# Expert routing with split one-hot products, slot weights as factors by partition, and six weight slabs fetched early

## The chip, the cores and the metric

One core of one Trainium2 chip runs the whole program in one launch. The metric is the device time of an execution in microseconds (us). A hardware profile of one execution comes with it.

## What is computed

Two transformer-like blocks on 512 tokens of 1024 channels, all float32. The change concerns one step of the first, the expert-choice feed-forward:

```python
def expert_choice_ffn(n, w_router, w_gate, w_up, w_down):
    cap = EC_FACTOR * L // N_EXPERTS                      # 64 of 512 tokens for each of 16 experts
    aff = jax.nn.softmax(jnp.einsum('bld,de->ble', n, w_router), axis=-1)
    vals, idx = lax.top_k(jnp.swapaxes(aff, 1, 2), cap)
    xs = jax.vmap(lambda hb, ib: hb[ib])(n, idx)          # gather
    a = jnp.einsum('becd,edf->becf', xs, w_gate)
    u = jnp.einsum('becd,edf->becf', xs, w_up)
    y = jnp.einsum('becf,efd->becd', jax.nn.silu(a) * u, w_down) * vals[..., None]
    return zeros(L, D).at[idx].add(y)                     # scatter
```

Before it stands a mixer with recurrences, behind it a norm and two layers of a second block (feed-forward, attention, feed-forward), which the change leaves alone.

## The kernel before, in words

The program is a row of stages, each a block with one instruction stream for each engine and a barrier behind it. Buffers hold 128 partitions; a tile of the token-major or channel-major activations is 128 x 512. Weights come as slabs of 128 x 2048 float32 (1 MiB), issued by SyncE. The function `experts` makes four stages of the feed-forward step:

- `route`: TensorE multiplies with the router (L104), VectorE makes the softmax and finds each expert's 64 tokens by eight rounds of maximum and replacement (L1426, L1427), and leaves in `slot_of` the slot of every token. SyncE loads the router and the tables for the later rotary embedding.
- `pick`: TensorE turns the normed activations to token-major form (L1488, 32 transposes), ScalarE copies them out as `x_tok` (L1470). VectorE compares slot numbers (L1442), which gives `pick`, a one-hot matrix of tokens by expert slots, and GpSimd multiplies it by the affinities (L1460), which gives `weighed`. Then the gather: 16 products of four float32 matmuls (L104 with `experts_work`), evicted in turn by VectorE and ScalarE into `xs`. Then 32 transposes of `weighed` (L1504) make `put`, by which the scatter multiplies.
- `experts`: eight pairs of experts, twelve slabs each, 96 in all, through a ring of eight slots. Gate and up (L1543), a transpose of the hidden tile (L1553), down (L1567), for two experts at a time in two halves of the array's columns. SyncE issues slab n when the pair of slabs eight before has been used (L1528). ScalarE evicts the result (L1589).
- `scatter`: for each of eight channel tiles eight float32 matmuls of `y` by `put` (L104), VectorE adds the tile to the residual (L1635), ScalarE squares it and GpSimd folds the squares (L156, L166) for the norm stage `final` that follows.

In the profile's names `experts_work` is the work buffer `m.work`, `mix_mixed` is lent for `xs`, and ring slots are `mix_ring` (4), `mix_normed` (2, the space of the normed activations) and `experts_work` (2). Where a float32 product is split, as in the feed-forward and projection stages, ScalarE writes a rounded copy of the operand in type fp32r (`hi`), VectorE subtracts it from the original (`lo`), and one matmul is made with each.

Of the kernel before, what the change touches and what calls it, by code (L numbers as in the profile page):

```python
# [14 lines left out]
F32 = mybir.dt.float32  # L15
# [7 lines left out]
P = 128  # L23
# [10 lines left out]
SG = 2  # L34
# [1330 lines left out]
def experts(nc, m, io):  # L1365


    w = m.work
    pick, weighed = cut(w, 0, NT, NE * CAP), cut(w, 4096, NT, NE * CAP)
    x_tok, put = cut(w, 8192, NT, D), cut(w, 12288, NE // 2, T)  # L1370
    small = 16384
    affinity, slot_of = cut(w, small, NT, NE), cut(w, small + 64, NT, NE)
    router = cut(w, small + 128, KD, NE)
    peak, total = cut(w, small + 256, NT), cut(w, small + 260, NT)
    top = cut(w, small + 264, 8)[0:NE]
    rest, chosen, ones_row, count = (cut(w, small + 288 + T * i, T)[0:NE] for i in range(4))
    xs = m.mixed[:, :, :].rearrange("p a b -> p (a b)").rearrange("p (k s) -> p k s", k=KD)
# [58 lines left out]
    with stage(nc, m, "pick") as (block, sem):  # L1436
        turned, copied, picked, weighted, gathered, put_done, freed, put_read = sem(8)

        @block.vector
        def _(dve):  # L1440
# [5 lines left out]
            for n in range(16):  # L1446
                dve.wait_ge(gathered, n + 1)
                k, half = divmod(n, 2)
                if n % 2 == 0:
                    dve.tensor_copy(xs[:, k, half * T:(half + 1) * T], m.ps[:, 4 + n % 4, :])\  # L1450
                        .then_inc(freed, 1)
            for pair in range(0, NE // 2, 2):
                dve.wait_ge(put_done, pair + 1)
                dve.tensor_copy(put[:, pair, :], m.ps[:, pair % 4, :]).then_inc(put_read, 1)

        @block.gpsimd
        def _(pool):
            for t in range(NT):
                pool.wait_ge(picked, t + 1)
                pool.tensor_tensor(weighed[:, t, :].rearrange("p (e s) -> p e s", e=NE),  # L1460
                                   pick[:, t, :].rearrange("p (e s) -> p e s", e=NE),
# [20 lines left out]
        def _(pe):  # L1482
            for n in range(8):
                if n >= 4:
                    pe.wait_ge(copied, n - 3)
# [1396 lines left out]
```

## Time and profile before

| | |
|---|---|
| median of 3 runs | 3973.25 us (3958.51, 3973.25, 3974.38) |
| profiled execution | 3963.0 us, of it the span 3961.1 us |
| TensorE busy | 3397.4 us, 86% of the span |
| VectorE, ScalarE, GpSimd busy | 1731.5, 1035.2, 268.6 us |
| granted TensorE clock, mean | 0.927 |
| DMA | 326.24 MB, mean 82 GB/s |

Times in rows are from the span's start. A float32 matmul leaves two records in the profile, an fp32r matmul one. PEclk is the granted TensorE clock as a share of 2.4 GHz. The records of matmuls overlap, so the pace of a burst is read from the starts. The idle time at a row's end was closed by the engine and line named behind it.

### The profile page before, as it was taken

To read this page: it belongs to the slowest core of one execution; us is meant where nothing else is said; L and a number is where in the kernel's file an instruction comes from. 1 tells how busy PE (TensorE), PEld (TensorE's weight loads), DVE (VectorE), ACT (ScalarE), POOL (GpSimd) and SP (SyncE) were. 2 spreads that over 40 slices of the span, in tenths; PEclk is the share of its full clock that TensorE was granted. 3 is DMA by queue.
4 is the path that set the end of the run, shared out by engine and by line. 5 is a ranking of instruction groups with operands and counts; after the bars stand their busy time and mean duration, and the time that the engine had idled before them with its cause. 6 is when DMAs were issued, how large, how long until landed. Compare 5 with 4: busy or idle time off the path is not lost. (4 is left out here: it accounts for less than half of the span.)

```text
span 3961.1 us, 39195 instructions
## 1 busy us (share of the span) xinstructions
PE 3397.4 (86%) x15298; PEld 2414.1 (61%) x15298; DVE 1731.5 (44%) x2473; ACT 1035.2 (26%) x1475; POOL 268.6 (7%) x230
## 2 busy tenths in 40 slices
PE   4988986768787778699978889999899798889997
PEld 3465665333463223588856457888788675557886
DVE  2747757464533000444234654442443235645433
ACT  2121221120321000422132453221322223443222
POOL 1110010020111000000001100000000102000001
PEclk6999998889888999799989899999999999899998
DMA  1101000101101993222121012221322121013221
GB/s 74 61 25 43 11 11 1 54 10 44 74 24 43 420 420 136 89 100 99 64 96 70 1 43 96 95 96 64 118 96 95 52 97 59 1 43 117 96 98 60
DMA packets 49390, 326.24 MB, mean 82 GB/s; under 512 B 6896, under 2 KB 7280, under 8 KB 11120
## 3 DMA queue, kind: packets, MB, share of 16 engines
q1 hardware_dynamic: 49264, 324.52, 21.7%
q8 instruction: 84, 1.38, 0.1%
q14 instruction: 42, 0.34, 0.0%
HBM read 321.35 MB, written 2.10 MB: 82 GB/s over the span
## 5 line engine op out<-in xcount | busy, mean ns | idle before, releaser
L358 PE MATMUL psum<-ffn_x_hi,ffn_w_hi 128*128 128x512 f32 x1408 | 551.4, 392 | 13.8 <-DVE ffn_x_lo L314 13.8
L358 PE MATMUL psum<-ffn_x_lo,ffn_w_hi 128*128 128x512 f32 x1408 | 550.9, 391 | 0.0
L358 PE MATMUL psum<-ffn_x_hi,ffn_w_lo 128*128 128x512 f32 x1408 | 550.5, 391 | 0.0
L303 DVE TENSOR_TENSOR ffn_w_lo<-ffn_raw,ffn_w_hi 128x2048 fp32r<-128x2048 f32 x128 | 293.4, 2292 | 420.8 <-ACT ffn_w_hi L274 420.8
L104 PE MATMUL psum<-mix_normed,mix_ring 128*128 128x512 f32 x832 | 373.9, 611 | 64.8 <-DMA mix_ring<-w_ssd 32.0
L274 ACT ACTIVATE ffn_w_hi<-ffn_raw 128x2048 fp32r<-128x2048 f32 x128 | 245.2, 1916 | 573.0 <-PE psum L358 573.0
L104 PEld LDWEIGHTS psum<-mix_normed,mix_ring 128*128 128x128 f32 x832 | 162.6, 197 | 273.3 <-issue 230.5
L358 PEld LDWEIGHTS psum<-ffn_x_hi,ffn_w_hi 128*128 128x128 f32 x1408 | 266.4, 189 | 75.2 <-DVE ffn_w_lo L310 20.0
L358 PEld LDWEIGHTS psum<-ffn_x_hi,ffn_w_lo 128*128 128x128 f32 x1408 | 266.1, 189 | 55.8
L358 PEld LDWEIGHTS psum<-ffn_x_lo,ffn_w_hi 128*128 128x128 f32 x1408 | 266.2, 189 | 55.6
L358 PE MATMUL psum<-ffn_hid_hi,ffn_w_hi 128*128 (+1 forms) x704 | 273.9, 389 | 0.0
L358 PE MATMUL psum<-ffn_hid_lo,ffn_w_hi 128*128 (+1 forms) x704 | 273.9, 389 | 0.0
L358 PE MATMUL psum<-ffn_hid_hi,ffn_w_lo 128*128 (+1 forms) x704 | 273.9, 389 | 0.0
L329 DVE TENSOR_TENSOR ffn_lift<-psum,squares_sb 128x512 f32<-128x512 f32 x88 | 60.8, 691 | 316.0 <-PE psum L358 316.0
L358 PEld LDWEIGHTS psum<-ffn_hid_hi,ffn_w_hi 128*128 128x128 f32 x704 | 132.1, 188 | 27.6
L358 PEld LDWEIGHTS psum<-ffn_hid_lo,ffn_w_hi 128*128 128x128 f32 x704 | 132.1, 188 | 27.5
L358 PEld LDWEIGHTS psum<-ffn_hid_hi,ffn_w_lo 128*128 128x128 f32 x704 | 132.1, 188 | 27.2
L624 DVE SCALAR_TENSOR_TENSOR recurrences_work<-psum,mix_group_cols,recurrences_work 128x509 f32<-128x509 f32 (+2 forms) x216 | 143.2, 738 | 0.0
L409 PE MATMUL psum<-mix_out_s_hi,mix_out_w_hi 128*128 128x512 f32 x256 | 103.0, 403 | 39.8 <-DVE mix_out_w_lo L460 39.8
L166 POOL TENSOR_TENSOR squares_sb<-squares_sb,ffn_gates 128x512 f32<-128x512 f32 x28 | 35.9, 1283 | 1457.2 <-ACT ffn_gates L156 1453.7
L409 PE MATMUL psum<-project_x_hi,project_w_hi 128*128 128x512 f32 x240 | 95.0, 396 | 46.2 <-DVE project_x_lo L1801 46.2
L292 ACT ACTIVATE ffn_hid_hi<-ffn_lift 128x512 f32 (+1 forms) x88 | 55.6, 632 | 267.7 <-DVE ffn_lift L333 267.7
(426 smaller groups left out, 5255.9 us busy)
## 6 DMA issues: line engine op xcount, KB each, us to landing
ffn_raw<-w_ffn SPq DMA_DIRECT2D x128, 1024.0 KB, 4.8
mix_ring<-w_experts SPq DMA_DIRECT2D x48, 1024.0 KB, 13.7
mix_ring<-w_mix SPq DMA_DIRECT2D x36, 1024.0 KB, 4.9
mix_normed<-w_experts SPq DMA_DIRECT2D x24, 1024.0 KB, 14.7
experts_work<-w_experts SPq DMA_DIRECT2D x24, 1024.0 KB, 15.7
mix_ring<-w_gdn SPq DMA_DIRECT2D x16, 1024.0 KB, 4.8
mix_ring<-w_ssd SPq DMA_DIRECT2D x10, 1024.0 KB, 6.9
mix_ring<-w_out SPq DMA_DIRECT2D x8, 1024.0 KB, 6.5
```

The lines of the kernel that those rows point to most:

```text
L104: ins = pe.matmul(out, weights(k), moving(k), start=(k == 0), stop=(k == n - 1))
L166: pool.tensor_tensor(m.squares, m.squares, tmp[:, k % 2, :], ALU.add).then_inc(folded, 1)
L274: act.activation(w_hi[:, q, :], raw[:, q, :], ACT.Copy).then_inc(hi_done, 1)
L292: act.activation(hid_hi[:, n, :], lift, ACT.Copy).then_inc(hid_hi_done, 1)
L303: dve.tensor_tensor(w_lo[:, q, :], raw[:, q, :], w_hi[:, q, :].bitcast(F32), ALU.subtract)\
L329: dve.tensor_tensor(lift, m.ps[:, 2 * q + 1, :], rstd, ALU.mult).then_inc(taken, 1)
L358: ins = pe.matmul(out, wp[:, q, w], xp, start=start and a == 0, stop=stop and a == 2)
L409: pe.matmul(out, a[0], b[0], start=start, stop=False)
L624: ins = dve.scalar_tensor_tensor(d[:, lo:hi], s[:, lo + shift:hi + shift], col[:, tap:tap + 1], d[:, lo:hi], ALU.mult, ALU.add)
```

## The change

1. `pick` and `put` are of type fp32r. The gathered activations are split: ScalarE's copy is `x_hi` (fp32r), VectorE subtracts to make `x_lo`, and the gather makes two fp32r matmuls where one float32 matmul stood. The scatter does the same with `y`, one channel tile at a time through two buffers, `y_hi` and `y_lo`.
2. GpSimd's weighting goes. `put` is the transpose of the bare one-hot matrix, and its transposes stand between the gather's products. The slot weights come from 32 float32 matmuls with two moving columns each, and become the factor `weight` of ScalarE's eviction in `experts`.
3. Slabs 0 to 3 are fetched in `route`, slabs 4 and 5 in `pick`, each with a semaphore of its own (`m.early`); the last two ring slots are a buffer that exists from `experts` on. The other 90 slabs are fetched in `experts` as before.
4. Memory: `m.mixed` lives only through the first mixer; the four stages get buffers of their own in place of the work buffer.

```diff
@@ -1365,16 +1365,25 @@
-    w = m.work
-    pick, weighed = cut(w, 0, NT, NE * CAP), cut(w, 4096, NT, NE * CAP)
-    x_tok, put = cut(w, 8192, NT, D), cut(w, 12288, NE // 2, T)
...
+    big = picking.enter_context(nc.sbuf_tensor("experts_pick", [P, 3 * 4096], F32R))
+    pick, x_hi, x_lo = (cut(big, 4096 * n, NT, NE * CAP) for n in range(3))
+    put = cut(m.moe_put, 0, NE // 2, T)
...
+    weight = cut(small, 6 * T, NE // 2)
+    xs = cut(m.moe_xs, 0, KD, NE * CAP)
+    spare = m.xT[:, :, :].rearrange("p k t -> p (k t)")
+    ring = [m.ring[:, s, :] for s in range(SLOTS)] + [spare[:, s * SLAB:(s + 1) * SLAB] for s in range(2)]
+    n_early = len(ring)
+
+    def fetch(sp, n):
+        sp.dma_start(ring[n], io["w_experts"][n]).then_inc(m.early[n], 16)
@@ -1384,6 +1393,8 @@
+            for n in range(SLOTS):
+                fetch(sp, n)
             sp.wait_ge(tables, 16)
@@ -1434,7 +1445,13 @@
     with stage(nc, m, "pick") as (block, sem):
...
+            sp.wait_ge(turned, 8)
+            for n in (4, 5):
+                fetch(sp, n)
@@ -1443,74 +1460,90 @@
                                   ALU.is_equal).then_inc(picked, 1)
+                for half in range(2):
+                    n, at = 2 * t + half, slice(half * T, (half + 1) * T)
+                    dve.wait_ge(hi_done, n + 1)
+                    dve.tensor_tensor(x_lo[:, t, at], m.ps[:, n % 4, :], x_hi[:, t, at].bitcast(F32), ALU.subtract)\
+                        .then_inc(split, 1)
...
+            dve.wait_ge(weighed, 1)
+            for e in range(2):
+                rows = slice(e * CAP, (e + 1) * CAP)
+                both = m.ps[rows, 4, 0:NE].rearrange("p (i e) -> p i e", e=2)
+                dve.tensor_copy(weight[rows], both[:, :, e])
-        @block.gpsimd
-        def _(pool):
-            for t in range(NT):
-                pool.wait_ge(picked, t + 1)
-                pool.tensor_tensor(weighed[:, t, :].rearrange("p (e s) -> p e s", e=NE),
...
             for n in range(8):
                 if n >= 4:
-                    pe.wait_ge(copied, n - 3)
+                    pe.wait_ge(split, n - 3)
...
-            pe.wait_ge(copied, 8)
+            pe.wait_ge(split, 8)
             pe.wait_ge(picked, NT)
             for n in range(16):
...
-                product(pe, m.ps[:, 4 + n % 4, :], lambda t: x_tok[:, t, tok(k)],
-                        lambda t: pick[:, t, half * T:(half + 1) * T], NT).then_inc(gathered, 1)
+                for t in range(NT):
+                    for part in (x_hi, x_lo):
+                        ins = pe.matmul(m.ps[:, 4 + n % 4, :], part[:, t, tok(k)], pick[:, t, half * T:(half + 1) * T],
+                                        start=(t == 0 and part is x_hi), stop=(t == NT - 1 and part is x_lo))
+                ins.then_inc(gathered, 1)
+                if n >= 5 and n % 2:
+                    turn_picks((n - 5) // 2)
+            turn_picks(6)
+            turn_picks(7)
+            pe.wait_ge(read_v, 7)
             for pair in range(NE // 2):
...
+                ins = product(pe, m.ps[:, 4, 2 * pair:2 * pair + 2], lambda t: pick[:, t, tok(pair)].bitcast(F32),
+                              lambda t: affinity[:, t, 2 * pair:2 * pair + 2], NT)
+            ins.then_inc(weighed, 1)
@@ -1522,7 +1555,7 @@
-            for n in range(12 * pairs):
+            for n in range(n_early, 12 * pairs):
                 if n >= slots:
@@ -1586,7 +1622,8 @@
-                    ins = act.activation(y[:, i, half * T:(half + 1) * T], m.ps[:, 5 + half, :], ACT.Copy)
+                    ins = act.activation(y[:, i, half * T:(half + 1) * T], m.ps[:, 5 + half, :], ACT.Copy,
+                                         scale=weight[:, i:i + 1])
@@ -1610,12 +1647,19 @@
         @block.scalar
         def _(act):
+            for k in range(KD):
+                if k >= 2:
+                    act.wait_ge(done, k - 1)
+                act.activation(y_hi[:, k % 2, :, :], y[:, :, tok(k)], ACT.Copy).then_inc(hi_done, 1)
             square_tiles(act, m, sq, renewed, squared, folded)
@@ -1625,14 +1669,28 @@
             for k in range(KD):
-                product(pe, m.ps[:, k, :], lambda pair: y[:, pair, tok(k)], lambda pair: put[:, pair, :],
-                        NE // 2).then_inc(done, 1)
+                pe.wait_ge(split, k + 1)
+                for pair in range(NE // 2):
+                    pe.matmul(m.ps[:, k, :], y_hi[:, k % 2, pair, :], put[:, pair, :], start=(pair == 0), stop=False)
+                    ins = pe.matmul(m.ps[:, k, :], y_lo[:, k % 2, pair, :], put[:, pair, :], start=False,
+                                    stop=(pair == NE // 2 - 1))
+                ins.then_inc(done, 1)
...
+            for k in range(KD):
+                dve.wait_ge(hi_done, k + 1)
+                dve.tensor_tensor(y_lo[:, k % 2, :, :], y[:, :, tok(k)], y_hi[:, k % 2, :, :].bitcast(F32),
+                                  ALU.subtract).then_inc(split, 1)
+                if k:
+                    add(k - 1)
+            add(KD - 1)
```

How it moves instructions, at three places. TensorE in `pick`, from the transposes of the activations to the stage's end, before:

```order
L65 UNCONDITIONAL_BRANCH
L1481 UNCONDITIONAL_BRANCH
L1488 MATMUL psum<-const_sb,mix_normed 128x128 x32
L104 MATMUL psum<-experts_work 128x512 x64
L1504 MATMUL psum<-const_sb,experts_work 128x128 x32
L65 UNCONDITIONAL_BRANCH
```

and with the change:

```order
L1503 UNCONDITIONAL_BRANCH
L1517 MATMUL psum<-const_sb,mix_normed 128x128 x32
L1527 MATMUL psum<-experts_pick 128x512 x48
L1509 MATMUL psum<-const_sb,experts_pick 128x128 x4
L1527 MATMUL psum<-experts_pick 128x512 x16
L1509 MATMUL psum<-const_sb,experts_pick 128x128 x4
...
L1527 MATMUL psum<-experts_pick 128x512 x16
L1509 MATMUL psum<-const_sb,experts_pick 128x128 x12
L104 MATMUL psum<-experts_small,experts_pick 128x2 x32
L65 UNCONDITIONAL_BRANCH
L1563 UNCONDITIONAL_BRANCH
```

Of the 32 transposes of the one-hot matrix 20 now stand inside the gather and 12 behind it; the 64 products are 128 matmuls, and 32 small ones close the stage. L1517, L1527 and L1509 are the lines of the activations' transposes, the gather and the one-hot transposes; `experts_pick` holds `pick`, `x_hi` and `x_lo`; the rows left out repeat the two above them.

SyncE from the router's transfer on, before:

```order
L1385 DMA experts_work<-w_router 128x128
L1386 DMA const_sb<-const_f 128x2304
L65 UNCONDITIONAL_BRANCH
L1523 UNCONDITIONAL_BRANCH
L1528 DMA mix_ring<-w_experts 128x2048 x4
```

and with the change:

```order
L1394 DMA experts_small<-w_router 128x128
L1395 DMA const_sb<-const_f 128x2304
L1385 DMA mix_ring<-w_experts 128x2048 x4
L65 UNCONDITIONAL_BRANCH
L1450 UNCONDITIONAL_BRANCH
L1385 DMA mix_normed<-w_experts 128x2048 x2
L65 UNCONDITIONAL_BRANCH
L1556 UNCONDITIONAL_BRANCH
L1561 DMA experts_slabs<-w_experts 128x2048 x2
```

Six slab transfers now stand ahead of the `experts` stage, four of them in `route`.

ScalarE in `scatter`, before and with the change:

```order
L1589 ACTIVATE experts_work<-psum 128x512 x4
L65 UNCONDITIONAL_BRANCH
L1617 UNCONDITIONAL_BRANCH
L156 ACTIVATE squares_sb<-resid_sb 128x512
L156 ACTIVATE mix_norm_tmp<-resid_sb 128x512 x7
```

```order
L1625 ACTIVATE experts_y<-psum,experts_small 128x512 x4
L65 UNCONDITIONAL_BRANCH
L1657 UNCONDITIONAL_BRANCH
L1662 ACTIVATE experts_y_hi<-experts_y 128x1024 x8
L156 ACTIVATE squares_sb<-resid_sb 128x512
L156 ACTIVATE mix_norm_tmp<-resid_sb 128x512 x7
```

Eight rounded copies now stand ahead of all eight squares in its queue.

## Rows read from the trace of the kernel before

**Rows 1.** The page, what DMA moved in 40 equal slices of the span, GB/s.

```profile
GB/s 74 61 25 43 11 11 1 54 10 44 74 24 43 420 420 136 89 100 99 64 96 70 1 43 96 95 96 64 118 96 95 52 97 59 1 43 117 96 98 60
```

**Rows 2.** Stretches of one stage each: length, busy us (instructions) by engine, PEclk, DMA share, GB/s.

```profile
1171.10:1206.60 35.50, 15.46 (x72) 14.60 (x72) 16.55 (x36) 1.54 (x2) 0.00 (x0) 0.50 0.10 36
1207.40:1275.00 67.60, 64.48 (x192) 33.40 (x192) 16.34 (x16) 11.63 (x20) 10.36 (x4) 0.97 0.00 0
1275.88:1523.90 248.02, 181.69 (x800) 64.22 (x800) 11.04 (x16) 14.74 (x25) 0.00 (x0) 0.98 0.98 406
1524.80:1584.50 59.70, 56.87 (x128) 24.83 (x128) 5.53 (x8) 5.03 (x8) 8.88 (x7) 0.97 0.00 0
```

**Rows 3.** Timeline of TensorE in pick: start us, us, line, what, count, idle before.

```profile
1207.47 5.81 PE L1488 MATMUL psum<-const_sb,mix_normed 128*128 128x128 f32 x32 [1.22 <-PEq L67]
1215.66 55.17 PE L104 MATMUL psum<-experts_work 128*128 128x512 f32 x128 [2.38 <-DVE experts_work L1442]
1270.67 3.66 PE L1504 MATMUL psum<-const_sb,experts_work 128*128 128x128 f32 x32
```

**Rows 4.** Timeline of SyncE and TensorE in experts.

```profile
1275.88 1.98 SPq L1528 DMA_DIRECT2D mix_ring<-w_experts  x4
...
1283.20 8.92 PE L1543 MATMUL psum<-mix_ring,mix_mixed 128*64 128x512 f32 x32 [8.87 <-DMA mix_ring<-w_experts]
1294.59 3.65 PE L1543 MATMUL psum<-mix_normed,mix_mixed 128*64 128x512 f32 x16 [2.47 <-DMA mix_normed<-w_experts]
...
1519.12 3.65 PE L1567 MATMUL psum<-experts_work 128*64 128x512 f32 x16 [1.28 <-DMA experts_work<-w_experts]
```

**Rows 5.** Timeline of scatter: TensorE, VectorE's last addition, GpSimd's last fold.

```profile
1524.85 56.87 PE L104 MATMUL psum<-experts_work 128*128 128x512 f32 x128 [2.08 <-PEq L67]
...
1581.76 0.69 DVE L1635 TENSOR_TENSOR resid_sb<-psum,resid_sb 128x512 f32<-128x512 f32 x1 [6.18 <-PE psum L104]
...
1583.19 1.26 POOL L166 TENSOR_TENSOR squares_sb<-squares_sb,mix_norm_tmp 128x512 f32<-128x512 f32 x1 [5.60 <-ACT mix_norm_tmp L156]
```

**Rows 6.** Timeline of TensorE in the projection, first and last of 39 fp32r matmuls.

```profile
2084.72 0.39 PE L409 MATMUL psum<-project_x_hi,project_w_hi 128*128 128x512 f32 x1
...
2093.33 0.39 PE L411 MATMUL psum<-project_x_hi,project_w_lo 128*128 128x512 f32 x1
```

**Rows 7.** The same kind at the start of a feed-forward stage, nine steps apart.

```profile
1620.52 0.63 PE L358 MATMUL psum<-ffn_x_hi,ffn_w_lo 128*128 128x512 f32 x1
...
1624.36 0.63 PE L358 MATMUL psum<-ffn_x_hi,ffn_w_lo 128*128 128x512 f32 x1
```

**Rows 8.** Single lines of code: durations ns min/median/max, first and last start, shapes.

```profile
L443 ACT ACTIVATE mix_out_s_hi<-mix_mixed x8: 1039/1061/1061, 1054.0 to 1131.3; 128x1024 fp32r<-128x1024 f32 x8
...
L457 DVE TENSOR_TENSOR mix_out_s_lo<-mix_mixed,mix_out_s_hi x8: 1218/1226/1226, 1055.1 to 1132.4; 128x1024 fp32r<-128x1024 f32 x8
...
L1442 DVE TENSOR_TENSOR experts_work<-const_sb,experts_work x4: 1217/2072/2924, 1207.5 to 1212.6; 128x1024 f32<-128x1024 f32 x4
...
L185 ACT ACTIVATE resid_sb<-resid_sb,gains_sb x6: 704/705/721, 1585.4 to 3936.7; 128x512 f32<-128x512 f32 x6
```

**Rows 9.** Short stretches for the clock: one-column products, end of router products, transposes.

```profile
138.00:140.00 2.00, 2.00 (x16) 1.64 (x14) 0.00 (x0) 1.23 (x2) 0.00 (x0) 1.00 0.67 131
...
1184.00:1188.00 4.00, 3.40 (x16) 3.29 (x16) 0.45 (x2) 0.00 (x0) 0.00 (x0) 0.50 0.00 0
...
1211.00:1213.00 2.00, 2.00 (x16) 2.00 (x15) 2.00 (x2) 1.58 (x4) 2.00 (x2) 0.79 0.02 4
```

**Rows 10.** Timeline of TensorE: one-column products, the router's products.

```profile
138.55 1.84 PE L780 MATMUL psum<-const_sb,mix_ring 128*128 128x1 f32 x16
...
1173.56 13.83 PE L104 MATMUL psum<-experts_work,mix_normed 128*128 128x16 f32 x64 [14.47 <-DMA experts_work<-w_router]
```

**Rows 11.** Timeline of the stage final: ScalarE's first square, GpSimd's folds.

```profile
1597.67 0.63 ACT L156 ACTIVATE squares_sb<-resid_sb 128x512 f32<-128x512 f32 x1 [5.30 <-DVE resid_sb L205]
...
1598.97 9.70 POOL L166 TENSOR_TENSOR squares_sb<-squares_sb,mix_norm_tmp 128x512 f32<-128x512 f32 x7 [14.52 <-ACT mix_norm_tmp L156]
```

More of the change, by code:

```diff
@@ L1365, in experts @@
 def experts(nc, m, io):
-    w = m.work
-    pick, weighed = cut(w, 0, NT, NE * CAP), cut(w, 4096, NT, NE * CAP)
-    x_tok, put = cut(w, 8192, NT, D), cut(w, 12288, NE // 2, T)
[L1371 to L1377, printed above, removed]
+    small = m.moe_small
+    picking, slabs, parts = ExitStack(), ExitStack(), ExitStack()
+    big = picking.enter_context(nc.sbuf_tensor("experts_pick", [P, 3 * 4096], F32R))
+    pick, x_hi, x_lo = (cut(big, 4096 * n, NT, NE * CAP) for n in range(3))
+    put = cut(m.moe_put, 0, NE // 2, T)
+    affinity, slot_of = cut(small, 0, NT, NE), cut(small, 64, NT, NE)
+    router = cut(small, 128, KD, NE)
+    peak, total = cut(small, 256, NT), cut(small, 260, NT)
+    top = cut(small, 264, 8)[0:NE]
+    rest, chosen, ones_row, count = (cut(small, 288 + T * i, T)[0:NE] for i in range(4))
+    weight = cut(small, 6 * T, NE // 2)
[5 more added lines that the diff above has]
+        sp.dma_start(ring[n], io["w_experts"][n]).then_inc(m.early[n], 16)
     by_expert = lambda a: a.unsqueeze(2).to_broadcast([P, NT, NE])
@@ L1611, in _ @@
                 dve.tensor_copy(hid_t[:, i % 2, :], m.ps[:, 4, :]).then_inc(turned_read, 1)
+    parts.close()
+    y_hi, y_lo = (parts.enter_context(nc.sbuf_tensor(f"experts_y_{n}", [P, 2, NE // 2, P], F32R))[:, :, :, :]
+                  for n in ("hi", "lo"))
     with stage(nc, m, "scatter") as (block, sem):
-        done, renewed, squared, folded = sem(4)
+        hi_done, split, done, renewed, squared, folded = sem(6)
         sq = cut(m.norm_tmp, 0, 2, T)
@@ L1627, in _, with add @@
             for k in range(KD):
-                product(pe, m.ps[:, k, :], lambda pair: y[:, pair, tok(k)], lambda pair: put[:, pair, :],
-                        NE // 2).then_inc(done, 1)
+                pe.wait_ge(split, k + 1)
[4 more added lines that the diff above has]
+                ins.then_inc(done, 1)
         @block.vector
         def _(dve):
-            for k in range(KD):
+            def add(k):
                 dve.wait_ge(done, k + 1)
                 dve.tensor_tensor(m.resid[:, k, :], m.ps[:, k, :], m.resid[:, k, :], ALU.add).then_inc(renewed, 1)
+            for k in range(KD):
[5 more added lines that the diff above has]
+            add(KD - 1)
+    parts.close()
+    slabs.close()
 MLA_H, NSA_H, SB_H = 6, 6, 4
@@ L2560, in memory @@
     m.signals = [ctx.enter_context(nc.semaphore(f"signal_{i}")) for i in range(48)]
+    m.early = [ctx.enter_context(nc.semaphore(f"expert_slab_{i}")) for i in range(SLOTS + 2)]
     m.ps = ctx.enter_context(nc.psum_tensor("psum", [P, 8, T], F32))
```

95 lines of the change are left out of this document (51 added, 44 removed).

## Prediction

> **What bounds the kernel now.** I read the page first, then the stretches stage by stage, then the timeline of each engine in three stages. The page's row of slices [rows 1] shows 420 GB/s in two of 40 slices and nothing near it elsewhere: one stage streams weights, and it is `experts`. The stretches [rows 2] give four stages that the diff touches. In `route` (35.5 us) TensorE runs at 0.50 of its clock and DMA moves 36 GB/s, so the memory port is nearly free. In `pick` TensorE is busy 64.5 of 67.6 us, in `scatter` 56.9 of 59.7: both are TensorE's. In `experts` DMA is at 0.98 while TensorE is busy 182 of 248 us.
>
> The timelines say what the work costs. In `pick` [rows 3] 64 float32 products stand as 128 records (each instruction leaves two) and take 55.17 us, 0.862 us a product; GpSimd's four weightings (10.36 us [rows 2]) lie beside the transposes and the start. In `experts` [rows 4] TensorE needs 3.65 us for a pair of slabs, but from the third pair (1294.59) to the last (1519.12) lie 45 steps of 4.99 us, each ended by a landing. In `scatter` [rows 5] the 64 products take 56.87 us, and behind them hang one addition (0.69), one square and one fold (1.27); the tail ends at 1584.45.
>
> **The price of a split product.** The projection stage has the same form, own weights for every 128x512 fp32r matmul: 38 steps from 2084.72 to 2093.33 [rows 6], 0.2266 us each. Two of them do what 0.862 us did, so a product costs 0.453 us. At the low clock the step is 0.427 us (nine steps in 3.84 us, 1620.52 to 1624.36 [rows 7]).
>
> **Pick: 68.4 us before** (1207.47 to the first issue of `experts`, 1275.88). Added on VectorE are eight subtractions between the four comparisons. A comparison took 1.22 us where nothing ran beside it and up to 2.92 beside GpSimd's multiplications [rows 8], which go; a 128x512 VectorE operation takes 0.69 [rows 5]. 4 x 1.22 + 8 x 0.69 = 10.4, with hand-offs to ScalarE I take 11.3 us until the first product (before: 8.2). What is queued behind that wait on TensorE is the whole gather. Then 128 x 0.2266 = 29.0 us of products, and the 32 transposes that were there before, 3.7 us [rows 3], now mostly between products; the evictions of both, about 0.7 us each, are shared by VectorE and ScalarE while a product of the gather takes 1.8 us, and stay hidden. At the start TensorE has been short of work and may begin at 1.2 GHz: `scatter` before began so and took 56.87 us where `pick` took 55.17, so 1.7 us [rows 3, 5], with 0 and 3.4 as ends. The transposes of `pick` did raise the clock, to a mean of 0.79 in 1211 to 1213 [rows 9]. The Trainium skill ("TensorE: Matmul & The Clock Gate", PE-mode transpose) says the reverse, that the full clock does not engage for transposes; by that rule this term would be 3.4 us instead of 1.7, and the trace does not agree with it here.
>
> New on TensorE are 32 float32 products with two moving columns, the slot weights, 64 records. Nothing covers them: the stage ends behind them. Their cost is that of loading 128x128 weights. Sixteen one-column products took 1.84 us at clock 1.00, 0.115 each; the router's 64 records took 13.83 us at 0.50, 0.216 each, and did not lift the clock in all that time [rows 9, 10]. So 7.4 us if the clock stays, 13.8 if it falls at once. They follow dense work, so it starts at 2.4 GHz and should fall on the way: I take the middle, 10.6. Two small copies and the hand-over: 1.4. Sum 11.3 + 1.7 + 29.0 + 3.7 + 10.6 + 1.4 = 57.7, **a gain of 10.7 us**. Ends: weights -3.2 and +3.2, start -1.7 and +1.7, comparisons still at their old median of 2.07 us +3.4, transposes in the stream somewhat dearer +1.2.
>
> **Experts: 249 us before.** Six slabs, three pairs, are in place when the stage starts, and the port has 45 pairs left for 48: -3 x 4.99 = -15.0 us [rows 4]. Cover for the six: four go out behind the router's and the rope tables' transfers in `route`, 10 us of port in a stage of 35.5 us whose port is idle after the tables [rows 2]; nothing in the stage waits for them, and the router's transfer stands ahead of them in the queue, so I charge 0 (at worst some 2 us). Two go out in `pick` after the eighth transpose group, with some 45 us of TensorE's work ahead. If that cover were gone, TensorE would wait at 4.99 us a pair as before. New is a possible hole: slabs 6 and 7 take the port for 5 us, slab 8 waits for the first pair's use. Before, two pairs took 8.92 us from the low clock, so the first 5.3 [rows 4]; reuse then comes at about the time at which the port runs dry. I charge 0.5 us, ends 0 and 3. An activation with a factor by partition takes 0.71 us [rows 8]; two stand behind the last pair, and I charge 0.2 us more than for plain ones. **Gain 14.3 us.** The Trainium skill ("DMA: Bandwidth & Descriptors", Where 436 GB/s comes from) puts the HBM side at about 358 GB/s; by that a slab would take 2.9 us and the six would be worth 17.6 us. The page's rows say 420 [rows 1], that is 2.5 us, and I go by them.
>
> **Scatter: 59.6 us before** (1524.85 to 1584.45). Before the first product now stand ScalarE's rounded copy, 1.06 us, and VectorE's subtraction, 1.23, on exactly these shapes [rows 8]: 2.5 with hand-offs. Then 29.0 us, and 2.0 for the low clock: TensorE ends at 33.5. Each tile is 3.63 us of TensorE. Its conversion starts when the tile two before is done and takes 2.5 us, VectorE's addition fits in between: hidden, slack 1.1 us. But ScalarE's squares stand behind all eight copies in its queue. The last copy is released with the sixth tile, at 33.5 - 7.3 = 26.2, and ends at 27.4. Then all eight squares and seven folds run in a row, as in the `final` stage, 1597.67 to 1608.67, 11.0 us [rows 11]: 38.4, and 0.5 more for folds beside VectorE: 38.9. So squares and folds, not products, end the stage, 2.7 us later than the old tail would. **Gain 20.7 us**, ends -2.5 and +2.7.
>
> **Sum.** 10.7 + 14.3 + 20.7 = 45.7 us. The profiled execution took 3963.0 us, so 3917.3 by itself. The runs shown lie on both sides of it (median 3973.25, 10.3 above); all four average 3967.3, and the forecast is taken from there: **3921 us**. The terms' bad ends together leave a gain of 32 us, the good ones 54; from the slowest run (3974.4) and the fastest (3958.5) that gives 3942 and 3904, the range. It takes in the two faster rivals below.
>
> **Rivals.**
> *Conversions bound the scatter* (chance 0.07). If copy and subtraction did not hide under the other tile, each of seven further tiles would add 2.5 us: 17.5, so 3939. For it: two buffers only, and VectorE's additions lie in the same queue. Against it: the slack of 1.1 us by rows 8.
> *The early slabs buy nothing* (0.06). If the port runs dry at the stage's start and stays behind, or the early fetches only move waiting: 14.3 us lost, 3936. The diff alone would allow it; the order of SyncE shows six issues ahead of the stage, and the rows show an idle port.
> *Products stay at 1.2 GHz* (0.03). If the gaps before both bursts kept the clock down, 256 x (0.427 - 0.227) = 51 us would be lost [rows 6, 7]: 3972, no change. Against it: the old bursts reached 0.97 on average over their stages [rows 2].
> *Slower: the one-hot operand forces the slow pace* (0.02). All 256 new matmuls take one fp32r operand and an fp32r one-hot matrix. If one operand made them run as float32, each would cost 0.862 instead of 0.227: 163 us more, 4084. It becomes slower than before by over 0.5% from 0.48 us a matmul on ((46 + 20) / 256 above 0.227). In the projection both operands are fp32r as well, and run at 0.227, which speaks against it.
> The forecast itself has 0.78; 0.04 is left for the first two together or something unseen, about 3950.
>
> **Chances.** About 0.5% (20 us) is what a measurement of this kernel can tell from no change. Below 3953 lie the forecast, the first two rivals and most of the remainder: 0.94. Within: 0.04. Slower: 0.02.
>
> **What would show it.** In the changed kernel's profile: fp32r records of `pick` and `scatter` 0.227 us apart; the first gather product some 11 us after the stage's start; the 64 small records in 7 to 14 us with the clock falling below 1.00; the first three pairs of `experts` with no wait, then steps of 4.99 us for 42 more and a stage some 14 us shorter; in `scatter` a VectorE subtraction always ended before the tile that needs it, and GpSimd's seven folds in a row ending some 5 us behind the last product. Wrong would be: products 0.43 us apart, waits of TensorE on the subtraction in `scatter`, a landing awaited in the first three pairs, or a first router product much later in `route` than now, 2.5 us after its start (1173.56 against 1171.10 [rows 2, 10]).

## The result, and the profile after

| | before | after |
|---|---|---|
| median | 3970.2 us (4 runs, 3958.51 to 3974.38) | 3914.91 us (4 runs, 3911.68 to 3919.42) |
| ratio | | 0.9867, 95% interval 0.9849 to 0.9885 |
| profiled execution | 3963.0 us | 3912.02 us, of it the span 3910.2 us |

The changed kernel is faster, by 1.3%. The prediction was 3921 us with a range of 3904 to 3942, and its forecast case came true. The stretches of the changed kernel, cut at the stages as in [rows 2], come first; the columns are length, busy time of the five engines with their instructions, granted clock, DMA share and GB/s. The stages are `route`, `pick`, `experts`, `scatter`.

```profile
1171.10:1206.60 35.50, 15.46 (x72) 14.60 (x72) 16.57 (x36) 1.54 (x2) 0.00 (x0) 0.50 0.39 154
1207.40:1262.90 55.50, 50.80 (x256) 44.12 (x256) 17.95 (x26) 11.52 (x20) 0.00 (x0) 0.87 0.10 39
1263.77:1498.60 234.83, 182.05 (x800) 64.48 (x800) 11.04 (x16) 16.17 (x25) 0.00 (x0) 0.99 0.97 402
1499.50:1538.20 38.70, 31.68 (x128) 25.18 (x128) 15.25 (x16) 13.09 (x16) 8.96 (x7) 0.93 0.00 0
```

`route` has its old length of 35.5 us although its DMA rate went up to 154 GB/s. `pick`, `experts` and `scatter` are shorter, and GpSimd has nothing left to do in `pick`. Measured from the stage's first transpose to the next stage's first slab issue, from there to ScalarE's first copy, and from there to the first scaling of the stage `final` (L185), the three take 56.28, 235.75 and 39.61 us, together 331.64. Before it was 377.96 us (1207.47 to 1585.43). So 46.3 us were saved there; the prediction had 45.7.

`pick`, in the timelines of TensorE and VectorE:

```profile
1207.49 4.91 PE L1517 MATMUL psum<-const_sb,mix_normed 128*128 128x128 f32 x24 [1.25 <-PEq L67]
...
1217.84 12.81 PE L1527 MATMUL psum<-experts_pick 128*128 128x512 f32 x48 [4.01 <-DVE experts_pick L1466]
1230.49 0.60 PE L1509 MATMUL psum<-const_sb,experts_pick 128*128 128x128 f32 x4
1230.84 3.93 PE L1527 MATMUL psum<-experts_pick 128*128 128x512 f32 x16
...
1251.02 1.47 PE L1509 MATMUL psum<-const_sb,experts_pick 128*128 128x128 f32 x12
1252.33 10.15 PE L104 MATMUL psum<-experts_small,experts_pick 128*128 128x2 f32 x64
```

```profile
1210.71 1.22 DVE L1459 TENSOR_TENSOR experts_pick<-const_sb,experts_small 128x1024 fp32r<-128x1024 f32 x1
1211.84 1.28 DVE L1466 TENSOR_TENSOR experts_pick<-psum,experts_pick 128x512 fp32r<-128x512 f32 x2
```

The gather's burst starts 10.35 us after the stage's start, released by VectorE's last subtraction. From there to the weights' products nothing is awaited. The 48 matmuls at the start take 12.65 us to the next record where 48 at the later pace of 0.2333 take 11.2. At the end the 64 small records take 10.15 us.

`experts` and SyncE's first issues in it:

```profile
1263.97 9.98 PE L1579 MATMUL psum<-mix_ring,experts_xs 128*64 128x512 f32 x32 [1.48 <-PEq L67]
1273.77 3.61 PE L1579 MATMUL psum<-mix_normed,experts_xs 128*64 128x512 f32 x16
1277.20 3.61 PE L1579 MATMUL psum<-experts_slabs,experts_xs 128*64 128x512 f32 x16
1280.63 7.22 PE L1579 MATMUL psum<-mix_ring,experts_xs 128*64 128x512 f32 x32
...
1289.19 3.65 PE L1579 MATMUL psum<-mix_normed,experts_xs 128*64 128x512 f32 x16 [0.75 <-DMA mix_normed<-w_experts]
...
1493.63 3.65 PE L1603 MATMUL psum<-experts_slabs,experts_small 128*64 128x512 f32 x16 [1.24 <-DMA experts_slabs<-w_experts]
```

```profile
1263.77 0.81 SPq L1561 DMA_DIRECT2D experts_slabs<-w_experts  x2
1270.54 4.24 SPq L1561 DMA_DIRECT2D mix_ring<-w_experts  x4
```

A pair of slabs is 16 matmuls. TensorE runs through six pairs without waiting for a landing; the seventh, at 1289.19, is the first that waits, and from there to the last pair lie 41 steps of 4.986 us, the pace of [rows 4]. The first slab of a reused place is issued at 1270.54, 6.8 us into the stage.

`scatter` by TensorE, ScalarE and GpSimd:

```profile
1501.88 0.78 PE L1674 MATMUL psum<-experts_put,experts_y_hi 128*128 128x512 f32 x1 [4.60 <-DVE experts_y_lo L1687]
1502.46 0.63 PE L1675 MATMUL psum<-experts_put,experts_y_lo 128*128 128x512 f32 x1
...
1505.41 0.39 PE L1674 MATMUL psum<-experts_put,experts_y_hi 128*128 128x512 f32 x1
...
1532.47 0.40 PE L1674 MATMUL psum<-experts_put,experts_y_hi 128*128 128x512 f32 x1
```

```profile
1526.14 1.06 ACT L1662 ACTIVATE experts_y_hi<-experts_y 128x1024 fp32r<-128x1024 f32 x1 [2.67 <-PE psum L1675]
1527.10 0.61 ACT L156 ACTIVATE squares_sb<-resid_sb 128x512 f32<-128x512 f32 x1
...
1528.32 9.83 POOL L166 TENSOR_TENSOR squares_sb<-squares_sb,mix_norm_tmp 128x512 f32<-128x512 f32 x7 [359.25 <-ACT mix_norm_tmp L156]
```

The first product stands 2.36 us after the first copy. Up to 1505.41 the records are 0.43 us apart, then 116 steps to 1532.47 take 27.06 us, 0.2333 each. From the fourth on, each copy waits 2.67 us for a tile of products, so ScalarE waits for TensorE and not the other way round. The squares stand behind the last copy, and the folds end at 1538.15, some 4.6 us after the last product.

**The rest of the span.** It fell by 50.9 us and the stages account for 46.3. The other 4.6 us lie behind the stages, in code that the change leaves alone (2375.7 us before, 2371.1 after). Below, e10_both_moves and e11_changed_again show one stretch of it taking either of two times, 3.8 us apart, with the new kernel alone. Whether the change makes the shorter time likelier is not shown.

### The profile page after: what moved, and what is told of

It reads as the page before. It is cut to its first block and busy times, and to the rows that moved or that the text cites. A ratio compares the mean times of both kernels' runs of the same rounds, so it can differ in the third digit from the quotient of the medians.

```text
span 3910.2 us, 39337 instructions
## 1 busy us (share of the span) xinstructions
PE 3354.9 (86%) x15362; PEld 2423.3 (62%) x15362; DVE 1743.4 (45%) x2491; ACT 1044.5 (27%) x1483; POOL 258.2 (7%) x226
```

## The experiments

The three parts were undone one by one (e1 to e3), the weights' products were left out (e8), the conversion's cover was taken away (e6), the order of the two passes changed (e7), and two pieces of work moved to where the new profile had room (e4, e5, and both in e10). The kernels of e1 to e8 ran once each, e10 and e11 five times. Whole spans drift by up to 5.5 us ahead of the four stages and up to 12 behind them, so I compare the stages' lengths and not the times of the whole. "Pick, experts, scatter" are those between the events named above.

**e1_fetch_in_experts: the six slabs fetched when the stage starts.**

```diff
             for n in range(SLOTS):
-                fetch(sp, n)
...
-            for n in (4, 5):
-                fetch(sp, n)
...
+            for n in range(n_early):
+                fetch(sp, n)
             for n in range(n_early, 12 * pairs):
```

> The changed kernel with all 96 slab transfers issued in the experts stage (six no longer ahead of it); nothing else moves. If the early slabs save port time: the experts stage, from its first issue to the start of scatter, grows from 235.8 us to about 249 us, as before the change, each of 45 steps from the third pair on 4.99 us; route, pick and scatter stay within 0.5 us; total near 3925. If the early slabs only moved waiting: experts grows by less than 3 us. If the fetches in routing disturbed the router or the picking: route or pick gets shorter than 35.5 and 56.3 us.

Measured: 3931.08 us. Pick 56.32, experts 249.08, scatter 39.60.

```profile
1269.30 2.05 SPq L1385 DMA_DIRECT2D mix_ring<-w_experts  x4
```

```profile
1276.70 9.72 PE L1573 MATMUL psum<-mix_ring,experts_xs 128*64 128x512 f32 x32 [8.68 <-DMA mix_ring<-w_experts]
1286.69 3.65 PE L1573 MATMUL psum<-mix_normed,experts_xs 128*64 128x512 f32 x16 [0.26 <-DMA mix_normed<-w_experts]
```

Without the early slabs TensorE waits for the first landing again, and `experts` has its old 249 us, 13.3 more than in the changed kernel. `pick` and `scatter` move by less than 0.1 us. From the router's transfer to `pick` it is 36.59 us here (1176.39 to 1212.98) and 36.35 with the slabs behind that transfer (1171.14 to 1207.49). So the early fetch is worth 13.3 us and costs nothing in `route`.

**e2_gather_float32: the gather by float32 products, without the split.** The one-hot matrices, the weights' products and the early slabs stay.

```diff
...
-                        ins = pe.matmul(m.ps[:, 4 + n % 4, :], part[:, t, tok(k)], pick[:, t, half * T:(half + 1) * T],
-                                        start=(t == 0 and part is x_hi), stop=(t == NT - 1 and part is x_lo))
+                ins = product(pe, m.ps[:, 4 + n % 4, :], lambda t: x_hi[:, t, tok(k)].bitcast(F32),
+                              lambda t: pick[:, t, half * T:(half + 1) * T].bitcast(F32), NT)
...
```

> The changed kernel with the gather alone back to float32: one float32 copy of the activations, no subtraction, 64 float32 products (128 records). If the price of a product is all: products take 55.2 us instead of about 30.5 with their slow start, but begin at 6.8 us into the stage instead of 10.4; pick goes from 56.3 to about 78 us, the other stages stay. If the conversion work of VectorE had eaten much of the gain, pick would grow by clearly less than 20 us.

Measured: 3938.07 us. Pick 76.36, experts 234.40, scatter 40.48.

```profile
1217.29 20.87 PE L104 MATMUL psum<-experts_pick 128*128 128x512 f32 x48 [0.79 <-ACT experts_pick L1485]
1238.00 0.60 PE L1504 MATMUL psum<-const_sb,experts_pick 128*128 128x128 f32 x4
```

The first product stands 6.66 us after the stage's start instead of 10.35, since the subtractions are gone, but sixteen records take 7.03 us where the split pass has 3.93. The stage is 20.1 us longer. So the split of the gather alone is worth more than `pick` gained in all: the weights' products gave about 9 us back. `experts` is 1.35 us shorter here. Its first pair was used by 1292.36, 5.4 us into the stage instead of 6.8, and the section on the prediction compares the port behind it. `scatter` is 0.9 us longer, and nothing was changed in it.

**e3_scatter_float32: the scatter by float32 products.** Copy and subtraction of this stage go with it.

```diff
-                    pe.matmul(m.ps[:, k, :], y_hi[:, k % 2, pair, :], put[:, pair, :], start=(pair == 0), stop=False)
-                    ins = pe.matmul(m.ps[:, k, :], y_lo[:, k % 2, pair, :], put[:, pair, :], start=False,
-                                    stop=(pair == NE // 2 - 1))
+                product(pe, m.ps[:, k, :], lambda pair: y[:, pair, tok(k)], lambda pair: put[:, pair, :].bitcast(F32),
+                        NE // 2).then_inc(done, 1)
```

> The changed kernel with the scatter alone back to float32: no rounded copies, no subtractions, 64 float32 products. Scatter, from its start to the last fold, goes from 38.7 us back to 59.6; the tail behind the last product goes from 5 us to 2.7; pick and experts stay within 0.5 us. Rival (conversions bound the scatter): less than 17 us.

Measured: 3944.72 us. Pick 56.36; experts and scatter together 294.5 instead of 275.4 us.

```profile
1502.84 55.17 PE L104 MATMUL psum<-experts_put,experts_y 128*128 128x512 f32 x128 [2.26 <-PEq L67]
```

The burst is as long as the old one of `pick` [rows 3]: this time it ran at the full clock throughout. To the next stage, from 1502.84, it is 58.9 us; the changed kernel has 39.6 from its first copy. By the two stages together, the split scatter is worth 19.1 us.

**e8_no_weight_products: the 32 two-column products left out.** The slot weights are set to 1, so the part of the computation that weights the experts' outputs is missing.

```diff
-            dve.wait_ge(weighed, 1)
...
+            dve.memset(weight, 1.0)
...
-            pe.wait_ge(read_v, 7)
-            for pair in range(NE // 2):
-                ins = product(pe, m.ps[:, 4, 2 * pair:2 * pair + 2], lambda t: pick[:, t, tok(pair)].bitcast(F32),
-                              lambda t: affinity[:, t, 2 * pair:2 * pair + 2], NT)
-            ins.then_inc(weighed, 1)
```

> The changed kernel without the 32 small slot-weight products and the two copies behind them; the factor is set to 1, so this part of the computation is left out. Theory: pick shortens by the 10.2 us of the products and some 0.3 more, 56.3 to about 45.8; TensorE comes from dense work into experts, its first pair takes 3.7 to 5.3 us instead of 6.5, and the hole in the port closes, experts shorter by 1 to 1.6 us. Rival (the low clock at the start of experts comes from the stage change, not from the small products): pick shortens alike, experts stays at 235.8.

Measured: 3900.05 us. Pick 46.98, experts 235.23, scatter 39.47.

```profile
1254.06 1.47 PE L1505 MATMUL psum<-const_sb,experts_pick 128*128 128x128 f32 x12
1257.27 7.09 PE L1570 MATMUL psum<-mix_ring,experts_xs 128*64 128x512 f32 x32 [1.74 <-PEq L67]
```

The products cost 9.3 us of `pick`, and behind them the clock is low: here the first two pairs take 7.09 us instead of 9.98. Only 0.5 us of these 2.9 reach the end of `experts`, where 1 to 1.6 were expected: the stage's pace is that of the landings.

**e4_weights_in_gather: these products in the gather, ahead of its last two groups.**

```diff
+                if n == 13:
+                    pe.wait_ge(read_v, 7)
+                if n in (13, 14):
+                    for pair in range(4 * (n - 13), 4 * (n - 12)):
+                        ins = product(pe, m.ps[:, 4, 2 * pair:2 * pair + 2],
...
-            pe.wait_ge(read_v, 7)
-            for pair in range(NE // 2):
```

> The changed kernel with the 32 slot-weight products moved between the gather's last products (16 behind the fourteenth, 16 behind the fifteenth, into the bank that is free by then), the last product and twelve transposes behind them. If the price of the small products is their pace at the low clock: spread in two bursts of 3.7 us the clock holds, they cost 64 x 0.115 = 7.4 us instead of 10.2, pick goes from 56.3 to about 53.5, and experts starts at the high clock as without the products (first pair 3.6 us, stage 235.2). If the clock falls anyway between the bursts: pick 55 to 57, and the products behind them run at 0.43.

Measured: 3911.45 us. Pick 55.28, experts 234.96, scatter 40.35.

```profile
1250.28 3.63 PE L104 MATMUL psum<-experts_small,experts_pick 128*128 128x2 f32 x32
1253.77 2.09 PE L1527 MATMUL psum<-experts_pick 128*128 128x512 f32 x8
1255.70 3.81 PE L104 MATMUL psum<-experts_small,experts_pick 128*128 128x2 f32 x32
1259.37 3.50 PE L1527 MATMUL psum<-experts_pick 128*128 128x512 f32 x8
```

In two lots between dense work they take 7.44 us instead of 10.15: the clock was 1.00 up to 1259. But the eight dense matmuls behind the second lot took 3.50 instead of 2.09 us, so the low clock came a little later and its 1.4 us moved to them. `pick` won 1.0 us, `experts` 0.8 (first pair at full clock, its place reused 3.9 us into the stage), and `scatter` lost 0.7, because its slow start lasted longer (up to 1508.27, twelve records). Over the three stages 1.05 us are left.

**e5_squares_between: each tile's square between two copies.**

```diff
...
+                if k >= 2:
+                    square(k - 2)
+            square(KD - 2)
+            square(KD - 1)
-            square_tiles(act, m, sq, renewed, squared, folded)
```

> The changed kernel with ScalarE's squares placed between its rounded copies in scatter (square of tile k-2 behind the copy of tile k) instead of behind all eight. If the squares' place in the queue ends the stage: the last fold ends some 2.7 us behind the last product instead of 4.6, scatter from its start to the next stage goes from 39.6 to about 37.6 us, products unchanged. If folds or conversions bound it in another way: no change, or waits of TensorE on the subtraction.

Measured: 3926.94 us. Pick 56.90, experts 235.56, scatter 37.62.

```profile
1536.31 1.29 POOL L166 TENSOR_TENSOR squares_sb<-squares_sb,mix_norm_tmp 128x512 f32<-128x512 f32 x1 [1.70 <-ACT mix_norm_tmp L1663]
1540.04 1.26 POOL L166 TENSOR_TENSOR squares_sb<-squares_sb,mix_norm_tmp 128x512 f32<-128x512 f32 x1 [2.44 <-ACT mix_norm_tmp L1663]
```

`scatter` is 2.0 us shorter and ends, as the old one did, with one addition, one square and one fold behind the last product: each fold now waits for its square. So the row of squares and folds was what ended the stage, and the copies still come in time, 3.73 us apart as before. The whole took longer all the same (span 3925.2 us against 3910.2), which the shorter stages cannot cause: 4.7 of these 15.0 us lie ahead of `pick`, whose first transpose stands at 1212.20 instead of 1207.49, and 11.8 behind the stages. e10 has the same move in five executions.

**e6_one_buffer: one pair of buffers for hi and lo in the scatter instead of two.** The conversion of a tile has to wait for the products of the tile before: its cover is gone.

```diff
-                if k >= 2:
-                    act.wait_ge(done, k - 1)
-                act.activation(y_hi[:, k % 2, :, :], y[:, :, tok(k)], ACT.Copy).then_inc(hi_done, 1)
+                if k >= 1:
+                    act.wait_ge(done, k)
+                act.activation(y_hi[:, 0, :, :], y[:, :, tok(k)], ACT.Copy).then_inc(hi_done, 1)
...
```

> The changed kernel with one buffer instead of two for the split tile of the scatter: a tile's copy and subtraction start when the product before has ended. Theory (two buffers hide 2.4 us a tile): scatter grows by 7 x 2.4 = 17 us, from 39.6 to about 56, less up to 2 us by which squares and folds then keep up; the clock may fall in the gaps and add more. Rival (conversions were on the path already): it grows by clearly less than 10.

Measured: 3949.96 us. Pick 56.32, experts 235.70, scatter 61.99. The waits of 1503 to 1566 (who waited for whom: total, times, longest):

```profile
ACT experts_y_hi L1662 <- PE psum L1675: 41.6, 7, 6.8
PEld psum L1674 <- DVE experts_y_lo L1687: 25.4, 8, 5.5
PE psum L1674 <- DVE experts_y_lo L1687: 21.4, 8, 4.6
```

Now TensorE waits eight times for the subtraction, 21.4 us in all, and the stage is 22.4 us longer. Its copies stand 6.40 us apart instead of 3.73, so an uncovered conversion costs 2.67 us. Two of the six distances were 7.80 and 7.74, since the clock dropped there. That is 16.0 and 2.7 us; the other 3.7 come from the last copy, which has the squares behind it in the queue and now waits for the seventh tile instead of the sixth. Only the second pair of buffers keeps the split scatter ahead: without it the stage takes 62.0 us, longer than the float32 one (58.9 in e3, 60.6 before).

**e7_hi_then_lo: in the gather all hi products of a group, then all lo ones.** It asks whether the measured pace, a little over the one forecast, comes from hi and lo taking turns.

```diff
-                for t in range(NT):
-                    for part in (x_hi, x_lo):
+                for part in (x_hi, x_lo):
+                    for t in range(NT):
```

> The changed kernel with the gather's matmuls in another order: four with the rounded part, then four with the rest, so that the moving operand changes with every matmul. In the changed kernel split products stand 0.2333 us apart in gather and scatter, where the projection has 0.2266. If the pace comes from two matmuls in a row with the same moving operand: 0.2266 in the gather here, pick 0.9 us shorter (128 x 0.0067), scatter still 0.2333. If it comes from the operands' layout or type: 0.2333 in both.

Measured: 3918.38 us. Pick 56.53, experts 235.64, scatter 39.43.

```profile
1221.14 12.82 PE L1527 MATMUL psum<-experts_pick 128*128 128x512 f32 x48 [4.00 <-DVE experts_pick L1466]
...
1234.15 3.93 PE L1527 MATMUL psum<-experts_pick 128*128 128x512 f32 x16
```

From the first product to the weights' products it takes 34.50 us (1221.14 to 1255.64), in the changed kernel 34.49 (1217.84 to 1252.33). The order does not matter. What sets 0.2333 instead of 0.2266 us stays open; the operands' layout was not tried.

**e10_both_moves (e4 and e5 together) and e11_changed_again (the changed kernel), five executions each on one chip.**

> The weights' products stand inside the gather (as in e4) and each tile's square stands between two hi copies of the scatter (as in e5). Theory: the two stretches do not touch each other, so the savings of the single runs add: pick 55.3 instead of 56.3 us, experts about 235, scatter to the next stage about 37.6 to 38.4 instead of 39.6, in all 2.5 to 4 us below the changed kernel, a median near 3911 where the changed one of the same call has 3914, and still 1.3 to 1.5% below the kernel before. Rival A: the saving is taken back behind the scatter (as the mixer of the second block drifts by 4 to 8 us from run to run, it could also drown): the medians of the two then agree within 1 us although the four stages are shorter. Rival B: the squares between the copies make ScalarE late for the subtraction; then the scatter's products pause between tiles and the stage is not under 39 us.

> The changed kernel once more, on the chip of e10 and against the same runs of the kernel before: pick 56.3, experts 235.7, scatter 39.6 us, together 46 us shorter than before; ratio 0.985 to 0.989. If what the whole span gained beyond these 46 us (4.6 us in the profiled pair) belonged to the change, the median would again be over 50 us below the kernel before; if it is drift of one profiled pair, the medians differ by more or less than that from call to call.

Measured: e10 3915.31 us (3911.98 to 3920.14), ratio to before 0.9864 (0.9847 to 0.9881). e11 3917.84 us (3915.27 to 3920.07), ratio 0.9870 (0.9855 to 0.9886). The stages: e10 57.34, 235.41 and 37.50, sum 330.25 us; e11 56.28, 235.78 and 39.56, sum 331.62. The squares' 2.0 us came again. The weights' move gained nothing in `pick` this time, and `pick` was 1.1 us longer. Some 0.4 of it is a slower start of the gather (13.07 us for the first 48 matmuls instead of 12.65); and the low clock fell on the dense matmuls behind the second lot and on the last twelve transposes, which took 2.74 us instead of 1.47.

```profile
1253.59 3.95 PE L104 MATMUL psum<-experts_small,experts_pick 128*128 128x2 f32 x32
1257.40 3.76 PE L1527 MATMUL psum<-experts_pick 128*128 128x512 f32 x8
1260.96 2.74 PE L1509 MATMUL psum<-const_sb,experts_pick 128*128 128x128 f32 x12
```

So the combined kernel is 1.4 us shorter in the stages, its median is 2.5 us lower, and the two intervals overlap: it is not shown to be faster than the changed kernel.

The same pair bears on the 4.6 us. Two issues of the second block's mixer, in the timelines of SyncE, of e10 first and e11 below:

```profile
2127.31 2.46 SPq L1962 DMA_DIRECT2D mix_work<-mix_projected  x4
...
2296.99 2.11 SPq L435 DMA_DIRECT2D mix_ring<-w_mix  x4
```

```profile
2127.05 2.46 SPq L1948 DMA_DIRECT2D mix_work<-mix_projected  x4
...
2292.92 2.10 SPq L435 DMA_DIRECT2D mix_ring<-w_mix  x4
```

Between them lie 169.68 us in one and 165.87 in the other, with the same instructions. Before and after show 169.64 (2174.58 to 2344.22) and 165.86 (2124.34 to 2290.20). The other eight traces fall on the same two times: 169.6 in e2, e3, e5 and e6, and 165.8 to 165.9 in e1, e4, e7 and e8. The granted clock tells them apart. These are the 30 us that begin 50 us into the stretch, before and after:

```profile
2224.58:2254.58 30.00, 26.43 (x119) 16.88 (x120) 15.43 (x44) 8.41 (x25) 0.00 (x0) 0.64 0.00 1
2174.34:2204.34 30.00, 26.05 (x140) 16.00 (x142) 18.95 (x57) 11.78 (x36) 0.00 (x0) 0.77 0.00 1
```

The six long stretches all have 0.64 there and the six short ones 0.77, and 0.13 of 30 us is 3.9 us, about the whole difference. What makes the clock take one course or the other is open. The stretch is also 3.8 of the 11.8 us by which e5 was longer behind the stages; the rest of those lies in other places. The changed kernel itself differs from one trace to the other: in e11 it took 2.8 us more than in the first ahead of `pick` and 3.3 more behind the stages.

The medians speak less clearly. By the expectation of e11, a median over 50 us below the kernel before would count for a gain of the change beyond its stages, and it was 50.7 us below (e10 53.2, the first four runs 55.3). So 4 to 9 us of the measured gain stand in none of the four stages. That the clock's course in one unchanged stretch makes 3.8 us is shown; that it is chance which kernel gets which course is not. Nor are the stages' lengths known for the executions without a trace: for the changed kernel two traces agree (331.64 and 331.62 us), for the kernel before there is one.

## Why the prediction was right

The forecast case was the one that happened, with 46.3 us in the stages for 45.7. The sum is nearer than its parts, whose misses partly cancel: `pick` gained 1.4 us more than forecast, `experts` 1.1 less. Its terms, in the order of the prediction:

| term | forecast | measured |
|---|---|---|
| pick: first gather product after | 11.3 us | 10.35 |
| pick: split products, pace | 0.2266 us | 0.2333 |
| pick: low clock at the start | 1.7 us | 1.4 |
| pick: the old 32 records of transposes | 3.7 us | 3.1 |
| pick: weights' products | 10.6 us | 10.15 |
| pick: gain | 10.7 us | 12.1 |
| experts: gain | 14.3 us | 13.2 |
| scatter: before the first product | 2.5 us | 2.36 |
| scatter: last product ends after | 33.5 us | 34.05 |
| scatter: last fold | 38.9 us | 38.6 |
| scatter: gain | 20.7 us | 21.0 |

**Pick.** The comparisons took 1.22 us each once GpSimd's multiplications were gone, the lower value of [rows 8] as assumed, and the subtractions 0.69: 10.4 us. VectorE waited 0.7 us for ScalarE in between, but its operations overlap at their ends by as much, so the 0.9 us of hand-offs that I had added on top are the excess. The pace term was 0.9 us too small over 128 matmuls. The 32 records of transposes that stand between the products and behind them cost 3.1 us (five times four at 0.35, the last twelve 1.31), not the 3.7 of [rows 3]. The weights' products stayed at clock 1.00 up to about 1256 and ended at 0.50, as the middle value assumed. e2 and e8 show the two large terms apart: 20.1 us for the split, 9.3 us back for the products.

**Experts.** e1 puts the six slabs at 13.3 us, and the steps of 4.986 us hold, so three pairs are 15.0 us less a hole. The mis-sized term is the hole, "0.5 us, ends 0 and 3": it was 1.6. In the prediction the reuse came 5.3 us into the stage, as in the kernel before, whose clock rose within the first pair (0.50 over 1283 to 1286, 0.77 over 1286 to 1288). In fact the clock stayed at 0.50 behind the two-column products up to 1269.8, and the reuse came at 6.8 us. The port, in 1 us stretches of the changed kernel:

```profile
1270.00:1271.00 1.00, 1.00 (x8) 0.37 (x6) 0.00 (x0) 0.00 (x0) 0.00 (x0) 1.00 0.24 98
1271.00:1272.00 1.00, 1.00 (x6) 0.31 (x4) 0.00 (x0) 0.00 (x0) 0.00 (x0) 1.00 0.94 131
1272.00:1273.00 1.00, 1.00 (x8) 0.40 (x6) 0.00 (x0) 0.00 (x0) 0.00 (x0) 1.00 0.65 262
```

Against 420 GB/s the three lines miss 1.8 us. Over the 5 us from 5 us into the stage on, the port misses as much (267 GB/s). In e2, where the reuse came at 5.4 us, it misses 0.5 there (380 GB/s), and that is the prediction's term at the prediction's moment: the step that failed is when the first place comes free, not what the port does then. In e4, e8 and e10, with the reuse at 3.9 us, it misses 0.9, 0.8 and 0.5 (347, 349 and 378 GB/s), so a still earlier reuse does not close the hole. The stage was shorter by 1.35 us in e2, 0.8 in e4, 0.5 in e8 and 0.3 in e10, which follows the hole only in part; what the rest is made of is not settled. The rule of the Trainium skill on the HBM side ("DMA: Bandwidth & Descriptors", Where 436 GB/s comes from) gave 17.6 us for the six slabs. The trace does not agree: the stage ran at 402 GB/s over its whole length, above the rule's 358. The slabs were worth 13.3 us.

**Scatter.** That the squares and folds, and not the products, end the stage was right and is shown by e5: take them out of the row, and the stage is 2.0 us shorter. It falls short of the 2.7 us by which the prediction had them later, since the products themselves ended 0.5 us later and the folds 0.3 earlier. The slow start held: eight records 0.43 us apart. The gain of 21.0 us has some luck in it: the burst before had a low clock near its start (0.62 over 1527 to 1530) and took 56.87 us where that of e3 took 55.17, and by e3 the split is worth 19.1.

**The rivals.** *Conversions bound the scatter* (0.07) did not happen, but its price was near: e6 takes the cover away, and TensorE's seven waits behind the first make 16.8 us (21.4 less 4.6) where the rival had 17.5. What the rival did not have is the clock, which dropped behind such pauses, and the squares, which were released a tile later. *The early slabs buy nothing* is refuted by e1. *Products stay at 1.2 GHz* did not happen: the clock was full again from about 1222 in the gather and from 1505.4 in the scatter. *The one-hot operand forces the slow pace* did not happen: 0.2333 us a matmul. The rule of the Trainium skill on transposes ("TensorE: Matmul & The Clock Gate", PE-mode transpose) would have given 3.4 us for the slow start of the gather; it was 1.4, since the clock had risen during the transposes, to 0.97 on average over 1212 to 1219, and fell back to 0.50 for 1219 to 1222 only, behind the wait of 4 us for the last subtraction.

**The level.** The forecast of 3921 stood 6 us over the measured median of 3914.91. The stages' 46.3 us do not explain that median: taken off the median of before (3970.2) they give 3923.9, off the profiled execution (3963.0) 3916.7. The sum had nothing for the stretches that the change does not touch, and the 9 us between the medians' gain and the stages' must lie there, if the stages took in every execution what the traces show. That the forecast came so near in spite of them is in part luck: it was taken from 3967.3 us for the time of before, 3 us under the median that was measured.

## What to carry to other kernels

A float32 product against a one-hot matrix can be made of two fp32r matmuls, hi and lo, at 0.47 us instead of 0.86, if the conversion of the next tile lies under the products of this one; with a single buffer the whole gain was gone (62.0 us against 39.6 with two and 60.6 before). Look then at what stood behind the old, slower engine: here a row of squares and folds at the end of ScalarE's queue became the tail, and work that only turned small (two-column products) took 10.15 us, in all of which weights were being loaded, and left the clock low for what followed. Fetches moved into a stage with an idle port are worth their landings at the streaming pace, less a hole that was 1.8 us with the first place free again at 6.8 us and 0.5 to 0.9 with it free at 3.9 to 5.4 us. And compare kernels stage by stage: unchanged code took two times here, 3.8 us apart, by the course of the granted clock.

## What the runs showed of the hardware that I had not expected

- The clock fell during a row of float32 products with two columns: 32 records took 3.63 us at 1.00, and of 64 in a row the last 28 ran at 0.50, 0.213 us apart instead of 0.112. Put between dense matmuls, they push the drop onto these (eight took 3.50 to 3.76 us instead of 2.09), so moving them saved 1.0 us once and cost 1.1 the next time.
- fp32r matmuls 128x512, each with weights of its own, stood 0.2333 us apart here and 0.2266 in the projection [rows 6], in either order of hi and lo.
- A burst of float32 products behind `experts` had a low clock near its start before (0.62 over 1527 to 1530, 56.87 us in all) and the full one throughout in e3 (55.17): the start is not the same in each trace.
- The same instructions of a later mixer took 169.6 us with the clock at 0.64 in one part of them and 165.9 us with 0.77, in six traces each.
- GpSimd's fold of 128x512 took 1.27 us on its own and 1.81 where it ran beside VectorE's subtraction (e10, the first five; one ran from 1513.74, a subtraction from 1513.18 to 1514.41). That the subtraction caused it was not tested.
